# Recurrence levels as 32-key products on four column groups, eight weight remainders moved to VectorE, attention probabilities turned by transposes

## The reference, cut to what matters

```python
p_s = masked_softmax(s_s, tok_ok[:, :, None])
o_s = jnp.einsum('bgrqn,bgqnd->bgrqd', p_s, vs_g)
...
return g_blk[..., 0:1] * o_c + g_blk[..., 1:2] * o_s + g_blk[..., 2:3] * o_w
```

```python
diff = bcum[..., :, None, :] - bcum[..., None, :, :]
dec = jnp.exp(jnp.where(causal, diff, -jnp.inf))
A = jnp.einsum('bhjc,bhsc,bhjsc->bhjs', qj, kj, dec)
o = jnp.einsum('bhjs,bhsv->bhjv', A, vj) + jnp.einsum('bhjc,bhcv->bhjv', qj * jnp.exp(bcum), Sst)
```

## Time and profile before

| what | value |
|---|---|
| median of three runs | 1008.73 us (1004.82 to 1010.64) |
| the profiled execution's own time | 1005.84 us |
| its span | 1004.0 us |
| TensorE matmul busy | 958.7 us, 95% |
| VectorE, ScalarE, GpSimd busy | 463.5, 542.2, 644.9 us |
| mean granted TensorE clock | 0.994 |

### The profile page before, as it was taken

How to read it: one execution, slowest core, us unless ns; L and a number is a source line. 1 busy time by engine, 2 the same in 40 slices (tenths; PEclk the granted TensorE clock), 3 DMA queues, 4 the chain that set the end, 5 groups by cost and what they waited for, 6 DMA issues and landing times.

```text
span 1004.0 us, 23104 instructions
## 1 busy us (share of the span) xinstructions
PE 958.7 (95%) x8988; PEld 917.6 (91%) x8988; DVE 463.5 (46%) x870; ACT 542.2 (54%) x799; POOL 644.9 (64%) x276
## 2 busy tenths in 40 slices
PE   5999999999989999999999999999999999999997
PEld 4988787899989979999999989999998899999996
DVE  5256423785744574433331133573584743334112
ACT  6577654575854676544434347676412654454441
POOL 2885324367799717877787756554413579878782
PEclk9999999999999999999999999999999999999999
DMA  8644222244543305555555544332002346555551
GB/s 338 208 155 146 65 85 84 85 129 150 164 139 113 127 22 189 168 170 177 175 183 162 180 148 147 127 116 95 3 3 87 104 148 211 186 181 181 185 182 50
DMA packets 39041, 139.79 MB, mean 139 GB/s; under 512 B 4272, under 2 KB 5552, under 8 KB 38832
## 3 DMA queue, kind: packets, MB, share of 16 engines
q1 hardware_dynamic: 38960, 138.62, 41.9%
HBM read 137.55 MB, written 1.05 MB: 138 GB/s over the span
## 4 chain that ended last, share of the span: by engine, by line
PE 56%; issue 23%; POOL 15%; DVE 3%; ACT 1%; DMA 1%; POOLq 0%; SPq 0%; DVEq 0%; ACTq 0%
PE ps L707 55%; POOL wlo L641 15%; DVE hT L1996 1%; DVE ivt L1969 1%; DMA ring<-in_stream 1%; POOL rN L682 0%; ACT whi L1529 0%; DVE mixT L1960 0%; DVE hA L2376 0%; DVE fxL L1960 0%; DVE aL L2006 0%; DVE wlo L1960 0%; PE ps L1260 0%; DVE aL L1969 0%; ACT rstd L1452 0%
## 5 line engine op out<-in xcount | busy, mean ns | idle before, releaser
L641 POOL TENSOR_TENSOR wlo<-ring,whi 128x1024 fp32r<-128x1024 f32 x251 | 600.6, 2410 | 316.7 <-ACT whi L1529 298.4
L1529 ACT ACTIVATE whi<-ring 128x1024 fp32r<-128x1024 f32 x253 | 266.8, 1060 | 162.9 <-PE ps L707 137.1
L707 PE MATMUL ps<-aH,whi 128*128 128x272 f32 (+1 forms) x1048 | 307.2, 293 | 10.8 <-POOL wlo L641 5.9
L707 PE MATMUL ps<-aH,wlo 128*128 128x272 f32 (+1 forms) x1048 | 300.9, 287 | 0.0
L707 PE MATMUL ps<-aL,whi 128*128 128x272 f32 (+1 forms) x1048 | 300.2, 286 | 0.0
L707 PEld LDWEIGHTS ps<-aH,whi 128*128 128x128 f32 x1048 | 199.9, 191 | 16.7 <-POOL wlo L641 7.4
L707 PEld LDWEIGHTS ps<-aL,whi 128*128 128x128 f32 x1048 | 199.9, 191 | 0.6 <-issue 0.5
L707 PEld LDWEIGHTS ps<-aH,wlo 128*128 128x128 f32 x1048 | 199.6, 190 | 0.0
L707 PE MATMUL ps<-fxH,whi 128*128 128x256 f32 x480 | 136.2, 284 | 4.3 <-POOL wlo L641 2.4
L707 PE MATMUL ps<-fxL,whi 128*128 128x256 f32 x480 | 135.8, 283 | 0.0
L707 PE MATMUL ps<-fxH,wlo 128*128 128x256 f32 x480 | 135.6, 283 | 0.0
(11 more groups left out here) (372 smaller groups left out, 1409.8 us busy)
## 6 DMA issues: line engine op xcount, KB each, us to landing
ring<-in_stream SPq DMA_DIRECT2D x253, 512.0 KB, 4.0
cst<-in_cst SPq DMA_DIRECT2D x1, 1325.0 KB, 12.7
xT<-in_x SPq DMA_DIRECT2D x4, 272.0 KB, 3.7
out<-hT SPq DMA_DIRECT2D x4, 256.0 KB, 2.4
row<-in_row SPq DMA_DIRECT2D x1, 898.0 KB, 9.5
cst<-in_cst SPq DMA_DIRECT2D x1, 640.0 KB, 10.3
mat<-in_mat SPq DMA_DIRECT2D x1, 576.0 KB, 13.6
vec<-in_vec SPq DMA_DIRECT2D x1, 135.0 KB, 3.8
```

The lines of the kernel that those rows point to most:

```text
L641: nc.gpsimd.tensor_tensor(wlo[:, s, :], ring[:, s, :], whi[:, s, :].bitcast(F32), ALU.subtract).then_inc(S("w_split"), 1)
L707: return nc.tensor.matmul(out, lhsT, rhs, start=start, stop=stop, skip_group_check=True)
L1529: nc.scalar.activation(whi[:, v % SLOTS, :], ring[:, v % SLOTS, :], ACT.Copy).then_inc(S("w_high"), 1)
```

## The change

- `level` is split. `diagonal` (level 0) forms 32x32 blocks on the diagonal, four to each of the sixteen blocks of tokens. `level` (1 to 7) multiplies 32 keys (64 at b = 64) only by the queries of the later halves. For b up to 16 these are four products of 32 keys by 16 queries each, on PSUM partitions 0, 32, 64 and 96, so in four column groups; for b = 32 two of 32 by 32; for b = 64 one of 64 by 64. The results are packed, eight blocks to a bank, so a level fits into banks 4 and 5 at once and needs no copy in between. `across` (level 8) uses banks 6 and 7.
- `banks_of` makes two masked copies of 512 elements in place of four of 256. Level 0 is a masked copy too, and hA is cleared by a memset before. From level 4 on the next level's `products` comes ahead of the copies; before only `products(8)` stood between copies.
- `V_LOW_AT`: the remainders of units 22, 23, 24, 25, 26, 28, 30 and 31 are made by VectorE (`low_of_unit`, L2354), behind units 18 to 27. GpSimd waits for them and passes `w_split` on.
- `turned` becomes transposes of the probabilities, which VectorE has weighted in place before (512 elements for p < 4, 1024 after); `diag` goes. At unit 18 VectorE does `attend(0)` ahead of the convolution, and `gated` moves to unit 16.

```diff
-V_LOW_AT = {}
-V_LOWS = tuple(V_LOW_AT.values())
+V_LOW_AT = {18: (22,), 20: (23, 24), 22: (25, 26), 24: (28,), 26: (30,), 27: (31,)}
+V_LOWS = sum(V_LOW_AT.values(), ())
...
+def copied_out(lev, bank):
+
+    return bank + 1 + (4 + 2 * (lev - 1) if lev else 0)
...
-                    m = mm(ps[:, 6, n * P:(n + 1) * P], prob[:, p % 2, g, kind * T + st * P:kind * T + (st + 1) * P],
-                           diag[:, p % 2, (2 * g + kind) * P:(2 * g + kind + 1) * P])
+                    m = nc.tensor.transpose(ps[:, 6, n * P:(n + 1) * P],
+                                            prob[:, p % 2, g, kind * T + st * P:kind * T + (st + 1) * P], C("ident"))
...
+            def diagonal():
+                pe.wait_ge(S("lev_qk"), 1)
+                for j in range(16):
+                    h, tok = j // 2, slice(j % 2 * P, (j % 2 + 1) * P)
+                    if j in (8, 12):
+                        pe.wait_ge(S("lev_a"), copied_out(0, j // 4 - 2))
+                    for q in range(0, P, 32):
+                        at = slice(tok.start + q, tok.start + q + 32)
+                        m = mm(ps[q:q + 32, 4 + j // 4 % 2, (j % 4) * P + q:(j % 4) * P + q + 32], fK[:, h, at], fQ[:, h, at])
+                    if j % 4 == 3:
+                        m.then_inc(S("lev_s"), 1)
...
             def level(lev):
-                q = qkl[:, lev % 2, :].rearrange("p (h t w) -> p h t w", h=8, t=2)
+
+                b, half = LEVELS[lev - 1], P // 2
+                keys, block = max(b, 32), max(2 * b, 32)
+                both = qkl[:, lev % 2, :].rearrange("p (j w) -> p j w", j=16)
                 pe.wait_ge(S("lev_qk"), lev + 1)
...
+                for j in range(16):
+                    if j % 8 == 0:
+                        pe.wait_ge(S("lev_a"), copied_out(lev - 1, j // 8 + (2 if lev == 1 else 0)))
+                    for q in range(0, P, block):
+                        later = both[:, j, q:q + block].rearrange("p (m w) -> p m w", w=2 * b)[:, :, b:]
+                        at = (j % 8) * half + q // 2
+                        out = ps[q:q + keys, 4 + j // 8, at:at + block // 2]
+                        m = mm(out.rearrange("p (m w) -> p m w", w=b), both[:, j, q:q + keys], later)
+                    if j % 8 == 7:
+                        m.then_inc(S("lev_s"), 1)
...
+                    if j in ATT_AT:
+                        attend(ATT_AT[j])
                     if j == 18:
                         convolved(j)
+                    if j == 16:
                         gated()
-                    if j in ATT_AT:
-                        attend(ATT_AT[j])
...
-                    tt(diag[:, p % 2, :].rearrange("p (n q) -> p n q", n=4), mid(C("ident"), 4), end(r, P), ALU.mult, "att_p")
+                    nk = P * (qt + 1)
+                    weights = prob[:, p % 2].rearrange("p g (k n) -> p (g k) n", k=2)[:, :, 0:nk]
+                    tt(weights, weights, end(r, nk), ALU.mult, "att_p")
...
+                step(nc.vector.memset(hA[:], 0.0))
...
+                        lev = LEVEL_AT[j]
+                        if lev == 0:
+                            diagonal_banks()
+                        elif lev < 4:
+                            banks_of(lev)
+                        products(lev + 1)
+                        if lev >= 4:
+                            banks_of(lev)
...
+                    for v in V_LOW_AT.get(j, ()):
+                        low_of_unit(v)
...
+                for j in range(2):
+                    dve.wait_ge(S("lev_s"), copied_out(lev, j))
+                    out = hA[:, 4 * j:4 * j + 4].rearrange("p h t (m w) -> p (h t) m w", w=2 * b)[:, :, :, b:]
+                    src = ps[:, 4 + j, :].rearrange("p (n m w) -> p n m w", n=8, w=b)
+                    step(nc.vector.copy_predicated(out, m.broadcast_to([P, 8, P // (2 * b), b]).bitcast(U32), src), "lev_a")
```

More of the change, by code:

```diff
@@ L1039, in hgrn_in @@
                         feature_tile(U_H + j, G_H + j, TM, ready)
-                    if j in LEVEL_AT:
+                    if LEVEL_AT.get(j) == 0:
+                        diagonal()
+                    elif j in LEVEL_AT:
                         level(LEVEL_AT[j])
+            def diagonal():
[9 more added lines that the diff above has]
+                        m.then_inc(S("lev_s"), 1)
@@ L1064, in hgrn, with across @@
+            def across():
+                q = qkl[:, 0, :].rearrange("p (h t w) -> p h t w", h=8, t=2)
+                pe.wait_ge(S("lev_qk"), 9)
+                for h in range(8):
+                    m = mm(ps[:, 6 + h // 4, (h % 4) * P:(h % 4 + 1) * P], q[:, h, 0, :], q[:, h, 1, :])
+                    if h % 4 == 3:
+                        m.then_inc(S("lev_s"), 1)
             def hgrn():
-                level(8)
+                across()
                 for h in range(8):
-                    if h in (0, 2):
-                        pe.wait_ge(S("lev_a"), 4 * 8 + h // 2 + 1)
+                    if h % 4 == 0:
+                        pe.wait_ge(S("lev_a"), copied_out(8, h // 4))
@@ L2361, in twice_gated, with diagonal_banks, banks_of @@
                 stt(out, out, 1.0, ps[:, g % MM_BANKS, 0:T], ALU.add, ALU.mult, "drained_v")
-            def banks_of(lev, banks):
-                for j in banks:
-                    dve.wait_ge(S("lev_s"), 4 * lev + j + 1)
-                    out = hA[:, 2 * j:2 * j + 2].rearrange("p h t w -> p (h t w)")
-                    src = ps[:, 4 + j % 2, :]
-                    if lev == 0:
-                        v = lambda ap: ap.rearrange("p (n w) -> p n w", n=4)
-                        tt(v(out), v(src), mid(C("ident"), 4), ALU.mult, "lev_a")
-                    else:
-                        b = LEVELS[lev - 1]
-                        v = lambda ap, n: ap.rearrange("p (n m w) -> p n m w", n=n, w=2 * b)[:, :, :, b:]
-                        m = v(C("hlev", 7 * P)[:, (lev - 1) * P:lev * P], 1).broadcast_to([P, 4, P // (2 * b), b])
-                        step(nc.vector.copy_predicated(v(out, 4), m.bitcast(U32), v(src, 4)), "lev_a")
+            def diagonal_banks():
+                for j in range(4):
+                    dve.wait_ge(S("lev_s"), copied_out(0, j))
+                    step(nc.vector.copy_predicated(hA[:, 2 * j:2 * j + 2].rearrange("p h t w -> p (h t) w"), mid(C("ident"), 4).bitcast(U32),
+                                                   ps[:, 4 + j % 2, :].rearrange("p (n w) -> p n w", n=4)), "lev_a")
+            def banks_of(lev):
+                b = LEVELS[lev - 1]
+                m = C("hlev", 7 * P)[:, (lev - 1) * P:lev * P].rearrange("p (n m w) -> p n m w", n=1, w=2 * b)[:, :, :, b:]
+                for j in range(2):
[3 more added lines that the diff above has]
+                    step(nc.vector.copy_predicated(out, m.broadcast_to([P, 8, P // (2 * b), b]).bitcast(U32), src), "lev_a")
             def products(lev):
@@ L2387, in hgrn @@
                 for j in range(2):
-                    dve.wait_ge(S("lev_s"), 4 * 8 + j + 1)
-                    step(nc.vector.tensor_copy(hX[:, 4 * j:4 * j + 4, :], ps[:, 4 + j, :].rearrange("p (h w) -> p h w", h=4)), "lev_a")
+                    dve.wait_ge(S("lev_s"), copied_out(8, j))
+                    step(nc.vector.tensor_copy(hX[:, 4 * j:4 * j + 4, :], ps[:, 6 + j, :].rearrange("p (h w) -> p h w", h=4)), "lev_a")
                 twice_gated(G_H + H_UNITS - 2, fZ[:, 6, :], "z_th", 6)
```

29 lines of the change are left out of this document (1 added, 28 removed).

## The result

The changed kernel took **997.89 us** (median of four runs, 996.27 to 999.85) beside 1009.68 us for the kernel before: ratio 0.9907, 95% interval 0.9881 to 0.9933, so 0.7 to 1.2% faster. Measured again later (`changed_again`) it was 996.57 us, ratio 0.9902 (0.9881 to 0.9923). Ratios are of fast executions; the one slow execution of all, 2119.95 us in `remainders_only`, is left out. The profiled execution took 997.6 us, its span 995.8 at a mean clock of 0.985. I had predicted 996.5.

The account below looks back on a forecast made before the run. TensorE's matmuls led the chain, with GpSimd full in the recurrence and VectorE the next bound. Recurrence -9.0, clock +1.7 and attention -5.0 made -12.3 us, from the median 1008.73 to 996.5 us (rounded), range 988 to 1004.5.

Parts of the forecast that it names:

- A level's price: In the recurrence, a level of 128 small records takes 1.5 us with entering and leaving the small shape, range 1.0 to 7.9.
- VectorE as the bound: In the recurrence, VectorE needs 7.95 us a stage against TensorE's 7.15, so VectorE is the bound.
- The exclusion with GpSimd: VectorE's two-input remainders wait out the GpSimd instruction they meet; each that gets in holds GpSimd 1.1 us; 3.5 us in all.
- over 1.3 where GpSimd works: Sign in the trace: VectorE's remainders recorded with over 1.3 us where GpSimd works, near 1.23 where it waits for them.
- The end of the chain: Recurrence's end: GpSimd to 331.5, last level's powers to 342.2, product to 343.5, copies to 345.7 instead of 354.70; gain 9.0 us.
- The clock: TensorE's new waits before level 7 and the cross product, about 3 us each, cost one clock fall: +1.7 us.
- late next: In the recurrence, level 7 (about 338.8) and the cross product get late, not the weights.
- The attention: Turns 2.0, idle before the first turn 1.62 and a clock fall 1.7: together 5.3, less 0.3, gain 5.0 us.
- Serial groups: Rival: column groups don't overlap, a level takes 4.2 us, TensorE stays the bound; total 1001 us; chance 0.13.
- No exclusion: Rival: no exclusion between VectorE and GpSimd, and quick copies; total 991 to 993 us; chance 0.17.
- No relief: Rival: each of eight remainders on VectorE waits a whole GpSimd instruction, and the counter with it; 1004 us; chance 0.10.
- The slower case: Rival: small records in the levels cost 0.062 us each, as the 30-column rows; 1027 us; chance 0.05.

Follow-up runs that it names:

- remainders_only: The kernel before with the eight remainders on VectorE alone, old levels and old attention: 1006.39 us, ratio 0.9991 to the kernel before.
- attention_only: The kernel before with the attention's part of the change alone: ratio 0.9975 to the kernel before.
- turns_only: The kernel before with weighting in place and transposes, VectorE's order at units 16 and 18 as before: ratio 0.9977 to the kernel before.
- gating_behind: The changed kernel with the gating back at unit 18, behind the first weighting and the convolution: 1001.15 us, ratio 0.9925 to the kernel before.

## Why the prediction was right, step by step

**Right in the whole, and the chain was the one named.** 996.5 predicted, 997.9 and 996.6 measured. On the profiled execution the sum said -12.3 and the trace shows 1005.84 - 997.6 = 8.2; by the medians' ratio it is 9.4. So the sum was about 3 us too large. That 996.5 lay so near is partly luck: it was reckoned down from 1008.73, and beside changed_again the kernel before took 1006.08. By attention_only (2.5 for 5.0) the excess lies in the attention; in the profile 1.6 us of it lie there, 1.5 are the fall at 222 us and 1.2 came behind the output products, where nothing was changed.

- **A level's price.** 1.5 us taken, 1.2 to 1.6 measured; the nearest rows by use of tiles were the right ones.
- **VectorE as the bound.** 7.95 us a stage predicted; its products for levels 2 and 3 began 8.05 apart, and it was busy 18.90 of 20 us.
- **The exclusion with GpSimd.** Remainders for which GpSimd waited took 1.24 each, two beside its work 3.29 and 1.49; GpSimd waited 3.00 and 3.81 us for VectorE's. My sign "over 1.3 where GpSimd works" was too simple: unit 22's remainder started 0.09 us ahead of a decay and took 1.23, and the decay paid instead, 2.89 us for 1.9 to 2.1.
- **The end of the chain.** On the clock of the changed kernel (1.86 us earlier) the last exponentials were predicted at 335.7 and came at 336.06, the last product at 340.3 and 340.67. The output products were predicted at 343.8 and came at 345.32: the fall that I had put behind their start came in the cross product, a step earlier.
- **The clock.** One fall of 1.7 us was charged; in the stretch there were three (285 to 291, 325 to 329 and 342 to 346 us at 0.72, 0.57 and 0.57), each behind a wait. By the waits, only the last lies on the path to the products; no run removes one of them alone. Stage gain 9.0 - 1.7 = 7.3 predicted, 7.5 measured from unit 17's weights. What I called "late next", level 7 and the cross product, was; level 5's 2.53 us I did not see coming: the fourth level's copies stood behind the 3.29 us remainder.
- **The attention, the mis-sized term.** "Together 5.3, less 0.3" became 3.4 at the mLSTM's rows in the profile and 2.5 in the total of attention_only. The 2.0 for the turns was right: 2.2 from the third turn on. Two other parts of the step failed. The wait of 1.62 before the first turn went, but it was no gain: the second turn waits for the second weighting, which ends at 104.8 us in turns_only and in gating_behind alike. And "the gating at unit 16 lies in VectorE's idle" was costed at nothing, though it holds GpSimd's port, and the copy behind it paid 0.9. The third part, 1.7 for the fall of the clock at 101 us, was left to chance. It did go there (101 to 105 at 1.00), but one stood at 97 to 101 (0.64) and another came at 222. The prediction saw one fall in the attention before; there were two, the other at 91 us, behind 5 us in which TensorE was recorded as busy throughout (columns as in the earlier trace rows):

```profile
85.00:90.00 5.00, 5.00 (x56) 4.76 (x55) 3.26 (x9) 3.71 (x6) 4.89 (x3) 1.00 0.64 201
90.00:95.00 5.00, 5.00 (x32) 4.76 (x32) 4.55 (x14) 2.23 (x9) 1.97 (x1) 0.66 0.65 212
```

**The rivals.** Serial groups: the order of products decides, and the kernel has the order that overlaps; serialised it gave 1003.9 where I had worked out 1001. No exclusion: refuted by 3.29 and 5.97 us. No relief: GpSimd's rest of a third from 300 to 320 us speaks against it, and the remainders bring 2.9 us of the stretch; but they bring them only with the short levels. The slower case needed 0.041 us a record; it was 0.009.

## What to carry to other kernels

When TensorE's part of a stage shrinks, ask for the chain through the other engines first: here 16 us off TensorE (the prediction's estimate) were worth 7.6 of the stretch, over a third of them only because GpSimd was relieved in the same change. Lay small products round the column groups in turn, never group by group. Never cost a VectorE instruction with two SBUF inputs at nothing because VectorE is idle: ask what GpSimd does then, and whether it leaves a gap. Before you move work out of one wait, look at the next thing its waiter needs: if that comes no earlier, the wait moves there. And compare stages between traces by a stretch without a fall of the clock, totals by medians.

## What the runs showed of the hardware that I had not expected

- GpSimd's instructions back to back can keep a VectorE instruction out for more than one of them: 5.97 us for work of 1.23, behind three. I had charged the rest of one. The Trainium skill (SBUF — State Buffer, Who interferes with whom) has the exclusion; that one side can lose several turns in a row is only in these rows. In the changed kernel it got in at 316 us after one whole GpSimd instruction and at 290 us ahead of one; each time the GpSimd instruction that then had to wait became about 0.9 us longer (2.96 for 2.04, 2.89 for 1.93).
- In these traces TensorE runs at half clock for 3.4, 6.8 or 10.2 us at a time, and behind the same wait of 1.99 us it does in one execution of the same kernel and not in another. It moved the mLSTM's rows between 162.7 and 165.0 us for one kernel, as much as the attention's whole change is worth. It doesn't always cost time: 3.4 us of it at 277 us, where TensorE waits much anyway (busy 3.37 of 7 us), changed the stretch around it by 0.03 us at most, those at 222 us cost 1.5.
